# Mixer weight residues kept in memory and the router's rows turned by VectorE

## The reference, cut to what matters

```python
h = layer_norm(x, ln_in_g, ln_in_b)                       # x is (1, 2048, 1024)
proj = h @ w_in                                           # 1024 -> 2048: v | gate B | gate C | u
pool_out = trailing means over 2/4/8/16 positions of v, minus v, then a 128x128 map per group
conv_out = B * (causal_depthwise_conv3(C * u) + bias)
h = layer_norm(ALPHA * h + concat(pool_out, conv_out) @ w_out, ln1_g, ln1_b)
probs = softmax(h @ w_router)                             # 1024 -> 16 experts, the router
# best of 4 expert groups, the top 2 experts in it, gates normalised
ffn = sum over the 2 experts of gate * ((silu(h @ w1[e]) * (h @ w3[e])) @ w2[e])
out = layer_norm(ALPHA * h + ffn, ln2_g, ln2_b)
```

## Time and profile before

| what | value |
|---|---|
| median of 3 runs | 1343.86 us (1342.79 to 1346.9) |
| the profiled execution's own time | 1346.83 us |
| span in its trace | 1344.7 us |
| PE busy | 1303.4 us (97%) |
| DVE busy | 993.2 us (74%) |
| ACT / POOL busy | 512.5 us / 523.2 us |
| DMA | 249.86 MB, mean 186 GB/s |

### The profile page before, as it was taken

One profiled execution on the slowest core, in us unless ns is written; L12 is line 12 of the kernel. 1 busy time (PEld: TensorE's weight loads), 2 busy tenths in 40 slices (PEclk: granted clock), 3 DMA queues, 4 the chain that ended last, 5 costly groups with the idle time before them and its releaser, 6 DMA issues.

```text
span 1344.7 us, 20326 instructions
## 1 busy us (share of the span) xinstructions
PE 1303.4 (97%) x6286; PEld 1086.2 (81%) x6287; DVE 993.2 (74%) x1382; ACT 512.5 (38%) x568; POOL 523.2 (39%) x555
## 2 busy tenths in 40 slices
PE   5999999999999999998999999999999999999995
PEld 5887888878887888887888888888888888888884
DVE  7769687797769885698777886775775677877574
ACT  3423234322432234324444454343442454443341
POOL 2001111121111110022566665656556556665655
PEclk9999999999999999999999999999999999999998
DMA  9626634763466444644877764563555545666421
GB/s 265 183 84 198 188 116 151 234 182 117 157 198 191 129 141 155 210 182 164 307 257 266 273 256 154 193 227 134 180 200 184 182 172 212 238 235 232 147 70 64
DMA packets 162858, 249.86 MB, mean 186 GB/s; under 512 B 19136, under 2 KB 91328, under 8 KB 162816
## 3 DMA queue, kind: packets, MB, share of 16 engines
q1 hardware_dynamic: 118624, 154.15, 34.6%
q0 software_dynamic: 30656, 78.03, 16.4%
q10 hardware_dynamic: 13536, 17.13, 3.8%
HBM read 218.26 MB, written 64.62 MB: 210 GB/s over the span
## 4 chain that ended last, share of the span: by engine, by line
PE 93%; DVE 3%; issue 1%; POOL 1%; DMA 1%; ACT 0%; SPq 0%; POOLq 0%; DVEq 0%; ACTq 0%
PE acc L530 28%; PE acc L532 28%; PE acc L531 28%; PE tp L578 3%; PE logits L612 2%; PE aux L839 1%; DMA b_in<-in_ln_in_b 1%; POOL small L1830 0%; DVE ring_lo L1259 0%; PE logits L658 0%; DVE ring_lo L1204 0%; DMA xg<-h_scratch,gat_now 0%; PE aux L532 0%; PE aux L531 0%; PE aux L530 0%
## 5 line engine op out<-in xcount | busy, mean ns | idle before, releaser
L530 PE MATMUL acc<-ring_hi 128*128 128x512 f32 (+1 forms) x800 | 308.5, 386 | 7.3 <-DVE hres L1334 4.7
L532 PE MATMUL acc<-ring_hi,ring_lo 128*128 128x512 f32 (+1 forms) x800 | 306.2, 383 | 0.0
L531 PE MATMUL acc<-ring_lo,ring_hi 128*128 128x512 f32 (+1 forms) x800 | 305.8, 382 | 0.0
L530 PE MATMUL acc<-ring_hi,xt_hi 128*128 128x512 f32 x648 | 257.0, 397 | 2.5 <-issue 2.4
L532 PE MATMUL acc<-ring_hi,xt_lo 128*128 128x512 f32 x648 | 252.9, 390 | 0.0
L531 PE MATMUL acc<-ring_lo,xt_hi 128*128 128x512 f32 x648 | 252.3, 389 | 0.0
L530 PEld LDWEIGHTS acc<-ring_hi 128*128 128x128 f32 x800 | 151.3, 189 | 37.6 <-issue 5.7
L532 PEld LDWEIGHTS acc<-ring_hi,ring_lo 128*128 128x128 f32 x800 | 151.1, 189 | 29.4
L531 PEld LDWEIGHTS acc<-ring_lo,ring_hi 128*128 128x128 f32 x800 | 151.3, 189 | 28.1
L1677 DVE TENSOR_TENSOR ring_lo<-stage_x,ring_hi 128x2048 fp32r<-128x2048 f32 x60 | 160.7, 2719 | 0.1
L1830 POOL TENSOR_TENSOR small<-small 128x1 f32<-128x1 f32 x31 | 47.4, 1530 | 280.7 <-DVE small L1218 280.7
(11 more groups left out here) (279 smaller groups left out, 1935.7 us busy)
## 6 DMA issues: line engine op xcount, KB each, us to landing
stage_x<-in_exp_w SPq DMA_DIRECT2D x64, 1024.0 KB, 4.8
stage<-in_w_in SPq DMA_DIRECT2D x64, 512.0 KB, 5.1
stage<-in_exp_w SPq DMA_DIRECT2D x32, 1024.0 KB, 6.5
stage<-in_w_out SPq DMA_DIRECT2D x32, 512.0 KB, 5.2
h_scratch<-hres POOLq DMA_DIRECT2D x16, 512.0 KB, 3.0
sum_scratch<-hres ACTq DMA_DIRECT2D x16, 512.0 KB, 2.9
hrow<-in_x POOLq DMA_DIRECT2D x12, 512.0 KB, 4.0
h_scratch<-hrow POOLq DMA_DIRECT2D x12, 512.0 KB, 3.6
```

The lines of the kernel that those rows point to most:

```text
L530: nc.tensor.matmul(dst, w_hi, x_hi, start=start, stop=False)
L531: nc.tensor.matmul(dst, w_hi, x_lo, start=False, stop=False)
L532: return nc.tensor.matmul(dst, w_lo, x_hi, start=False, stop=stop)
```

## The change

The residues of the 12 mixer units are made once. In chunk 0 DVE splits as before, and SP stores each residue (1 MB) in `lo_dram`; in chunks 1 to 3 SP loads them from there into `ring_lo` instead of DVE making them (36 splits fewer, 12 stores and 36 loads more). PE then waits on ACT's cast and on the load. SP's loads of a unit wait on ACT's cast of an earlier unit instead of on DVE's split.

The router's rows of chunks 0 to 2 are not transposed by PE. ACT scales and stores the rows two units behind the norm (j = 2 to 5), reads the stored h1 rows back as four quarter loads three units behind it (j = 3 to 6, `h1_back`) and DVE turns them with one 32x32 transpose of 1024 elements (`h1_turn`, j = 3 to 6). `route_tile` stands between the two sections of units 4 to 7. The router's weights are laid out `(p k)` instead of `(k p)`, and the last chunk's transposes, still on PE, read with a stride to match.

`residual(c, 0, 0)` goes from the head of DVE's unit 10 into unit 9 in chunks 0 to 2.

```diff
+            def keep_lo(u):
+                sp.dma_start(lo_dram[u], ring_lo[:, u % RING1, :].bitcast(F32)).then_inc(s_kept[u % RING1], 16)
+            def back_lo(u):
+                if u < CU + RING1:
+                    sp.wait_ge(s_kept[u % RING1], 16 * (CU // RING1))
+                sp.dma_start(ring_lo[:, u % RING1, :].bitcast(F32), lo_dram[u % CU]).then_inc(s_back[u % RING1], 16)
...
-            for c in range(1, NCH):
-                for j in range(CU):
-                    sp.wait_ge(s_lo, c * CU + j - 1)
-                    load_mixer(j)
+                else:
+                    keep_lo(j - 2)
+            for u in range(CU, MU):
...
+                else:
+                    sp.wait_ge(s_hi, u - 1)
+                    load_mixer(u % CU)
+                    back_lo(u - 2)
...
+                        if not first and which == 0 and j >= 4:
+                            route_tile(c - 1, j - 4)
...
-                    if not first:
-                        if 3 <= j < 7:
-                            route_tile(c - 1, j - 3)
-                        if 2 <= j < 6:
-                            h1_tile(c - 1, j - 2)
...
+            def h1_back(c, t):
+                act.wait_ge(s_ahout[t], c * 16 + 16)
+                rows = h1_dram[(c * TPC + t) * P:(c * TPC + t + 1) * P, 0:D].rearrange("(r b) (a f) -> a r b f", r=SUB, a=QUARTERS)
+                for a in range(QUARTERS):
+                    dst = hres[a * SUB:(a + 1) * SUB, t, :].rearrange("r (b f) -> r b f", b=QUARTERS)
+                    act.dma_start(dst, rows[a]).then_inc(s_h1q[t], 16)
...
-                    if not first and 3 <= j < 7:
-                        h1t_copy(c - 1, j - 3)
-                    if not first and 4 <= j < 8:
-                        alpha_h1(c - 1, j - 4)
+                    if not first and 2 <= j < 6:
+                        alpha_h1(c - 1, j - 2)
+                    if not first and 3 <= j < 7:
+                        h1_back(c - 1, j - 3)
...
             def unit_ahead(c, j, last):
                 ja = j + RING1 - 1
-                if ja >= CU and last:
+                if c * CU + ja >= CU:
                     return
+                if ja >= RING1:
+                    dve.wait_ge(s_kept[ja % RING1], 16 * (ja // RING1))
                 split_lo(ja % 2, c * CU + ja + 1, ja % RING1)
...
+            def h1_turn(c, t):
+                dve.wait_ge(s_h1q[t], (c + 1) * 16 * QUARTERS)
+                dve.wait_ge(s_log, c * TPC + t)
+                if c >= 1 and t == 0:
+                    dve.wait_ge(s_lst, c)
+                V.transpose(h1t[:].rearrange("p k (r b) -> p k b r", r=SUB),
+                            hres[:, t, :].rearrange("p (b c k) -> p k b c", b=QUARTERS, c=SUB)).then_inc(s_h1turn, 1)
...
                     if j < 8 and j % 2 == 1:
                         gate_rows(c, g)
+                    if not first and 3 <= j < 7:
+                        h1_turn(c - 1, j - 3)
...
                         if j == 9:
+                            residual(c, 0, 0)
                             ln_h(c + 1, 2, nth())
```

More of the change, by code:

```diff
@@ L120, in build @@
     w2_v = exp_w2[0].rearrange("(g i) (k p) n -> i g p k n", p=P, g=NEG)
+    lo_dram = nc.dram_tensor("lo_scratch", (CU, P, UNIT), F32).ap()
     with ExitStack() as ctx:
@@ L361, in build @@
         s_lo = sem("unit_lo")
+        s_kept = [sem(f"slot{i}_lo_stored") for i in range(RING1)]
+        s_back = [sem(f"slot{i}_lo_loaded") for i in range(RING1)]
         s_used = sem("unit_used")
@@ L394, in build @@
         s_h1t = sem("h1_transposed")
+        s_h1q = [sem(f"h1_quarters_in{t}") for t in range(TPC)]
+        s_h1turn = sem("h1_quarters_turned")
         s_h1tc = sem("h1_t_copied")
@@ L496, in _ @@
                     x_first(j + 2)
-            for c in range(1, NCH):
-                for j in range(CU):
-                    sp.wait_ge(s_lo, c * CU + j - 1)
-                    load_mixer(j)
+                else:
+                    keep_lo(j - 2)
+            for u in range(CU, MU):
+                if u < CU + 2:
+                    sp.wait_ge(s_lo, u - 1)
+                    load_mixer(u % CU)
+                    keep_lo(u - 2)
+                else:
+                    sp.wait_ge(s_hi, u - 1)
+                    load_mixer(u % CU)
+                    back_lo(u - 2)
+            for u in range(MU, MU + 2):
+                sp.wait_ge(s_hi, u - 1)
+                back_lo(u - 2)
             def load_expert(ex, j):
@@ L509, in _ @@
                 if j < 2:
-                    sp.wait_ge(s_lo, MU - 1 + j)
+                    sp.wait_ge(s_hi, MU - 1 + j)
                 elif j == 4:
@@ L532, in three, with unit_split @@
                 return nc.tensor.matmul(dst, w_lo, x_hi, start=False, stop=stop)
+            def unit_split(u):
+                if u < CU:
+                    pe.wait_ge(s_lo, u + 1)
+                else:
+                    pe.wait_ge(s_hi, u + 1)
+                    pe.wait_ge(s_back[u % RING1], 16 * ((u - CU) // RING1 + 1))
             def unit_cols(slot, lo, n):
@@ L598, in pool_map @@
                     .then_inc(s_pm, 1)
[L600 to L605, removed]
             def route_tile(c, t):
-                pe.wait_ge(s_h1tc, (c * TPC + t + 1) * 2)
+                pe.wait_ge(s_h1turn, c * TPC + t + 1)
                 tile = (c * TPC + t)
@@ L646, in h1_ready @@
                 elif t >= 2:
-                    pe.wait_ge(s_h1tc, (LAST * TPC + t - 1) * 2)
+                    pe.wait_ge(s_h1tc, (t - 1) * 2)
             def h1_last(t, k):
-                mm = nc.tensor.transpose(last_banks[t % 2][k // 4][:, k % 4, :], hres[:, t, k * P:(k + 1) * P], ident[:])
+                by_k = hres[:, t, :].rearrange("p (c k) -> p k c", k=KT)
+                mm = nc.tensor.transpose(last_banks[t % 2][k // 4][:, k % 4, :], by_k[:, k, :], ident[:])
                 if k % 4 == 3:
@@ L655, in route_last @@
                 if k % 4 == 0:
-                    pe.wait_ge(s_h1tc, (LAST * TPC + t) * 2 + k // 4 + 1)
+                    pe.wait_ge(s_h1tc, t * 2 + k // 4 + 1)
                 tile = LAST * TPC + t
@@ L691, in chunk @@
                     g = j // 2
-                    pe.wait_ge(s_lo, c * CU + j + 1)
+                    unit_split(c * CU + j)
                     if j == 0:
@@ L747, in chunk @@
                 if last:
-                    pe.wait_ge(s_lo, c * CU + CU)
+                    unit_split(c * CU + CU - 2)
+                    unit_split(c * CU + CU - 1)
                     for t in range(TPC):
@@ L968, in route_exp @@
                 nc.scalar.activation(rt[c].prob[:], rt[c].shift[:], ACT.Exp).then_inc(s_exd, 1)
[L970 to L976, removed]
             def alpha_h1(c, t):
                 act.wait_ge(s_h1out[t], c * 16 + 16)
-                act.wait_ge(s_h1t, (c * TPC + t + 1) * 2)
+                if c == NCH - 1:
+                    act.wait_ge(s_h1t, (t + 1) * 2)
                 nc.scalar.mul(hres[:, t, :], hres[:, t, :], ALPHA).then_inc(s_ah, 1)
@@ L984, in alpha_h1 @@
                 act.dma_start(sum_dram[bass.ds((c * TPC + t) * P, P), :], hres[:, t, :]).then_inc(s_ahout[t], 16)
+            def h1_back(c, t):
[4 more added lines that the diff above has]
+                    act.dma_start(dst, rows[a]).then_inc(s_h1q[t], 16)
             def res_load(c, t):
+                act.wait_ge(s_h1turn, (c - 1) * TPC + t + 1)
                 act.wait_ge(s_ahout[t], c * 16)
@@ L998, in load_consts @@
                 act.dma_start(pw_raw, pool_w[0].rearrange("g c d -> c g d")).then_inc(s_const, 16)
-                act.dma_start(wr[:], w_router.rearrange("(k p) e -> p k e", p=P)).then_inc(s_const, 16)
+                act.dma_start(wr[:], w_router.rearrange("(p k) e -> p k e", p=P)).then_inc(s_const, 16)
                 act.dma_start(g_1[:], bc(ln1_g[0])).then_inc(s_const, 16)
@@ L1087, in _ @@
                 for b in range(2):
-                    act.wait_ge(s_h1t, ((NCH - 1) * TPC + t) * 2 + b + 1)
+                    act.wait_ge(s_h1t, t * 2 + b + 1)
                     if t >= 2:
@@ L1246, in h_turn @@
                 dve.wait_ge(s_xq[t % 2], ((c - 1) * 2 + t // 2 + 1) * 16)
-                if t == 0 and c > 1:
-                    dve.wait_ge(s_h1tc, (c - 1) * TPC * 2)
                 dve.wait_ge(s_trlo, (c * TPC + t) * 2)
@@ L1469, in chunk @@
                     if j == 10:
-                        for t in range(TPC):
+                        for t in range(0 if last else 1, TPC):
                             residual(c, 0, t)
```

## The result

The kernel after takes **1368.07 us** (median, 1365.1 to 1373.07); the kernel before, beside it, 1345.34. The ratio is **1.0173, 95% interval 1.0157 to 1.0189**: the change makes the kernel 23 us slower, where I had forecast 1339.0. The profiled execution's span went from 1344.7 to 1371.3 us.

The account below looks back on a forecast made before the run. PE, with 93% of the chain, was taken as the bound. Gains of 17.9 us, less 9.6 of router waits and 3.4 of slow clock, gave -4.9: from 1343.9 to 1339.0 us, range 1331 to 1348.

Parts of the forecast that it names:

- the waits at unit 4: First tile's router, chunks 1 to 3: PE waits 3.2 us each for DVE's turn, 9.6 us in all.
- Transposes: 96 router transposes leave PE's path, 12 tiles at 0.79 us: gain 9.5 us.
- unit 10: Its head in chunks 1 and 2: the late residual's gap and slow clock go, gain 2 x 4.2 = 8.4 us.
- Router waits at the other tiles: Tiles 1 to 3: none expected; the turns come 1.4, 2 and 1.4 us before PE asks.
- the walk: DVE's order in chunk 1 in old times: free at 208.33, turn ends 210.6, PE asks at 207.38.
- the covered transfers: Residue stores and loads and quarter loads run beside PE's path; residue loads are issued three units (33 us) early; no cost.
- the rival of the chain at a chunk's end: Last input tile's store and read-back land late behind bursts, PE waits at chunk heads: 9 to 14 us, chance 0.13.
- The likeliest case: Waits only at unit 4, part of them followed by slow clock; 1336 to 1342 us, chance 0.45.
- the clock: Behind the three unit 4 waits: two falls in three, 1.7 us each, 3.4 us in all.
- My bound of 5.1: Upper bound in us of the clock loss behind the unit 4 waits; the lower bound was 0.
- ACT's term: Four quarter-load issues of about 0.4 us a tile; ACT reaches its acc[2] copy 0.5 us later, still before DVE wants it.

Follow-up runs that it names:

- e_hold: Kernel after, with SP holding unit 11's burst (stage unit and residue) until the last input tile is read back: 1360.85 us, ratio 1.0105.
- e_both: Kernel after, with the router's matmuls behind the second section of units 4 to 7 and unit 11's burst held until the last input tile's read-back: 1332.78 us.
- e_best: e_both, with the residue load of unit 10's burst also held behind the last input tile's read-back: 1330.36 us, ratio 0.9879.
- e_lohold: e_lo, with SP holding unit 11's burst until the last input tile is read back: 1344.47 us, ratio 0.9994.
- e_spq: Kernel after, with the first tile's four quarter loads issued by SP instead of by ACT in unit 3: 1363.49 us, ratio 1.0110.
- e_resid: Kernel before, with only residual(c, 0, 0) moved into unit 9: 1342.06 us, ratio 0.9982.
- e_turnlate: Kernel before plus DVE's router turn and the moved residual, router's matmuls behind the second section of units 4 to 7, no residues from memory: 1333.10 us.
- e_lo: Kernel before plus residues from memory and the moved residual, router's rows still transposed by PE: 1345.98 us, ratio 1.0003.
- e_fill: Kernel after, with 20 unread matmuls of 512 columns on PE before the first tile's router in unit 4 of chunks 1 to 3: 1356.02 us.

## Why the prediction was wrong

The sum failed on a term that it put at nothing, the landings at the chunk ends, and on two that it held too small; the waits at unit 4 came by the mechanism that it gave.

**The gains were right.** Transposes 9.5 forecast, 10.3 measured; unit 10 8.4 forecast, 8.5 measured. Router waits at the other tiles, which the walk excluded, came once (0.8 us in chunk 3, with 1.7 of clock).

**First step that failed: the covered transfers, with the rival of the chain at a chunk's end.** The likeliest case put the residues' transfers at nothing. I gave the rival 0.13 and argued that bursts are issued at the head of a unit and the read-back near its end. I took the time of SP's bursts from the kernel before, although I had written myself that SP now waits on ACT and issues earlier. Before, the burst came at 299.47, 3.1 us behind the read-back's issue and 0.9 us ahead of the ranks' matmuls in unit 11 (300.34). In after it comes 3.3 us ahead of them (298.11 and 301.42), and the read-back, late by its own store, is issued behind it. The two landings grew by 9.3 us, where 5 were to bring a wait and 6 a loss, and chunk ends cost 18.0 us, above my price of 9 to 14. I reasoned with the mean DMA share, 0.70 rising to near full (the same stretch after, 282 to 306, shows 0.84), and the landings went by what was in the queues in front of them: e_hold, e_both and e_best move the same bytes in another order and lose most of the wait, e_best all of it. The Trainium skill ("DMA: Bandwidth & Descriptors", Queues, rings and completion order) says that an engine takes turns between its queues packet by packet. How long a transfer of 0.5 MB then stays behind a burst of 2 MB does not follow from that alone. Here it landed with the burst's last load, 309.17 and 309.83, after 3 us in which the engines served SP's queue alone; for the third tile in e_lohold the two landed 1.5 and 0.6 us apart. It is not always so: the second tile's read-back there, issued 0.15 us behind a residue load (263.91 and 263.76), landed 4.6 us ahead of it (270.82 and 275.46).

**Second: the clock, 3.4 us in the sum.** I priced each fall at the 1.7 us of the earlier trace rows, and took two falls in three. All three router waits were followed by one, and they cost 4.1, 3.1 and 4.5, 11.8 together: 8.4 us too little, the largest error in a term that the sum had. The other three falls (2.8, 2.6 and 1.7) came with waits that the sum did not hold. My bound of 5.1 was three times the one size that I had seen, so the term's range was not a range. That the size was wrong also at the forecast's length of wait shows e_spq: behind its three waits of 3.2 us the falls cost 3.5, 3.5 and 1.8.

**Third: the wait in unit 4, 3.2 each forecast, 4.3 to 4.6 measured.** The mechanism and DVE's walk were right, as e_spq shows. Mis-sized was ACT's term: four issues at 0.4 us, taken from a store's 0.34. A quarter load takes 0.66 to 0.79, so ACT came to its copy 1.4 us later than DVE's walk allowed, not before it. In the sum this is 3.7 us, 13.3 for 9.6.

Together: 12.1 (unit 4 with its clock, 25.1 for 13.0) + 18.0 + 2.5 - 0.9 (gains) = 31.7, the distance from -4.9 to +26.8.

## What to carry to other kernels

Before traffic is added to a queue, lay the latency-critical transfers of the other queues over its issue times, in the order that the *new* waits give, and not over a mean share; a transfer issued right behind 2 MB at a chunk's end here landed with the last of it, and holding the burst back behind that transfer brought no wait for a weight in e_both or e_best. A turn that is needed in the same unit as its inputs appear should be asked for one section later: that alone was worth 24.6 us of the loss here. Taking 80 us from an engine that is not the bound was worth about 3.

## What the runs showed of the hardware that I had not expected

- **Issuing costs the issuer more for quarter loads.** The 48 on ACT took 0.55 to 0.92 us each, median 0.68; its plain stores of 512 KB took 0.34.
- **Granted clock and gaps do not go by length alone.** PE was idle for 1.6 us at two chunk heads of e_resid and of e_turnlate, and 2.9 us once in e_lo, with no slow clock behind. In e_lo the same idle time 148 us later did bring it:

```profile
301.00:305.00 4.00, 4.00 (x20) 3.29 (x19) 3.97 (x7) 1.17 (x2) 1.69 (x3) 1.00 1.12 312
...
449.00:453.00 4.00, 4.00 (x12) 3.09 (x12) 3.93 (x8) 1.18 (x2) 0.77 (x1) 0.59 1.17 279
```

  Gaps of 0.4 us (e_both), 0.5 (e_hold), 0.59 (e_fill) and 0.62 (after, chunk 3) in front of the router's 16 matmuls of 16 columns were followed by a fall; one of 0.56 (e_spq, chunk 3) and one of 0.25 (e_best) were not. These traces give no rule for it.
- **The 32x32 turn keeps its price per element when doubled.** 1024 elements in one instruction took 2.06 to 2.29 us, mean 2.21, about twice the 1157 ns for 512 of the earlier trace rows, though it writes SBUF where that one writes PSUM.
